# Modulation vectors of two MLP stages: from TensorE with a 32-column weight tile to VectorE with a running sum; squares of every MLP from VectorE to ScalarE

## The reference

```
silu_c, silu_cc = silu(c), silu(c_ctx)                    # two condition vectors of 1024
for i in range(4):
    sh_a, sc_a, g_a, sh_m, sc_m, g_m = split(silu_c @ mod_w[i] + mod_b[i], 6)        # mod_w[i]: 1024 x 6144
    csh_a, ... = split(silu_cc @ mod_w[i] + mod_b[i], 6)                             # layers 0 to 2 only
    h = rms_norm(x, g) * (1 + sc_a) + sh_a                # mixer: Fourier, differential attention, MLA, Fourier
    x = x + g_a * mixer(h)
    x = x + g_m * (square(relu(h2 @ mlp_w1[i])) @ mlp_w2[i])     # h2 modulated by sh_m, sc_m; hidden width 4096
```

## Time and profile before

| what | value |
|---|---|
| median of three runs | 3288.2 us (3286.24 to 3288.66) |
| the profiled execution | 3285.3 us |
| its span | 3284.0 us |
| TensorE matmul busy | 3151.4 us, 96% |
| VectorE busy | 1728.4 us, 53% |
| ScalarE busy | 1393.5 us, 42% |
| GpSimd busy | 998.6 us, 30% |
| granted TensorE clock, mean | 0.989 of 2.4 GHz |

### The profile page before, as it was taken

The page is one execution under the profiler, slowest core; times in us unless marked ns, Lnnn a source line. Parts: engine busy times, 40 slices in busy tenths (PEclk is TensorE's granted clock), DMA queues, the critical chain, the costliest instruction groups (busy, mean ns, idle before and its releaser), DMA issues.

```text
span 3284.0 us, 52135 instructions
## 1 busy us (share of the span) xinstructions
PE 3151.4 (96%) x21802; PEld 2675.0 (81%) x21802; DVE 1728.4 (53%) x3037; ACT 1393.5 (42%) x2347; POOL 998.6 (30%) x440
## 2 busy tenths in 40 slices
PE   5999999999999999999999999999999999999999
PEld 3877777776777777589989987778999978779999
DVE  3353333666543334666566556564466556554574
ACT  3442222444432223654444445554344446554443
POOL 0212113110212212134423432343434423334443
PEclk8999999999999999999999999999999999999999
DMA  9345454332355553135525542333545433325454
GB/s 290 111 155 162 155 166 154 116 103 90 105 190 167 171 175 103 54 119 189 177 79 180 179 131 74 107 95 103 173 145 184 157 103 103 103 91 164 150 180 149
DMA packets 469306, 460.07 MB, mean 140 GB/s; under 512 B 9041, under 2 KB 467665, under 8 KB 469073
## 3 DMA queue, kind: packets, MB, share of 16 engines
q1 hardware_dynamic: 465760, 453.32, 43.2%
q10 hardware_dynamic: 3312, 3.42, 0.3%
HBM read 455.66 MB, written 1.05 MB: 139 GB/s over the span
## 4 chain that ended last, share of the span: by engine, by line
PE 76%; DVE 14%; ACT 6%; issue 3%; DMA 1%; ACTq 0%; POOL 0%; DVEq 0%; SPq 0%; POOLq 0%
PE bank L400 21%; PE bank L401 20%; PE bank L402 20%; ACT wh L347 3%; DVE wl L363 3%; PE bank L444 3%; DVE hl L779 1%; DVE hidl L779 1%; DVE tmp L665 1%; PE bank L2388 1%; PE bank L563 1%; DVE xl L673 1%; DVE bc L2428 1%; PE bank L458 1%; PE bank L1250 1%
## 5 line engine op out<-in xcount | busy, mean ns | idle before, releaser
L375 POOL TENSOR_TENSOR wl<-raw,wh 128x768 fp32r<-128x768 f32 (+2 forms) x336 | 880.4, 2621 | 2101.0 <-ACT wh L347 2091.0
L347 ACT ACTIVATE wh<-raw 128x2048 fp32r<-128x2048 f32 (+1 forms) x336 | 636.4, 1894 | 315.0 <-PE bank L402 298.6
L363 DVE TENSOR_TENSOR wl<-raw,wh 128x1280 fp32r<-128x1280 f32 (+2 forms) x336 | 499.7, 1487 | 420.5 <-ACT wh L347 411.7
L400 PE MATMUL bank<-nh,wh 128*128 128x272 f32 (+1 forms) x1712 | 506.5, 296 | 6.3 <-DVE nl L1973 2.8
L402 PE MATMUL bank<-nh,wl 128*128 128x272 f32 (+1 forms) x1712 | 494.2, 289 | 0.0
L401 PE MATMUL bank<-nl,wh 128*128 128x272 f32 (+1 forms) x1712 | 492.6, 288 | 0.0
L400 PE MATMUL bank<-xh,wh 128*128 128x512 f32 (+1 forms) x1288 | 449.8, 349 | 6.9 <-DVE xl L673 3.7
L401 PE MATMUL bank<-xl,wh 128*128 128x512 f32 (+1 forms) x1288 | 437.8, 340 | 0.0
L402 PE MATMUL bank<-xh,wl 128*128 128x512 f32 (+1 forms) x1288 | 437.0, 339 | 0.0
L400 PE MATMUL bank<-hh,wh 128*128 128x512 f32 (+1 forms) x1024 | 350.3, 342 | 3.7 <-DVE X L687 1.9
L400 PEld LDWEIGHTS bank<-nh,wh 128*128 128x128 f32 x1712 | 326.7, 191 | 23.2 <-issue 19.6
(11 more groups left out here) (424 smaller groups left out, 5634.4 us busy)
## 6 DMA issues: line engine op xcount, KB each, us to landing
raw<-in_mlp_w SPq DMA_DIRECT2D x128, 1024.0 KB, 5.3
raw<-in_mod_w SPq DMA_DIRECT2D x83, 1024.0 KB, 5.2
raw<-in_w_in SPq DMA_DIRECT2D x60, 1024.0 KB, 5.2
raw<-in_w_mlp_up SPq DMA_DIRECT2D x32, 1024.0 KB, 5.5
raw<-in_w_mlp_down SPq DMA_DIRECT2D x32, 1024.0 KB, 5.0
raw<-in_w_in SPq DMA_DIRECT2D x34, 512.0 KB, 4.3
raw<-in_w_ssd_down SPq DMA_DIRECT2D x16, 1024.0 KB, 5.1
early<-in_mod_w SPq DMA_DIRECT2D x13, 1024.0 KB, 12.0
```

The lines of the kernel that those rows point to most:

```text
L347: nc.scalar.activation(self.wtile(self.wh, c1), self.rawtile(c1), AF.Copy).then_inc(*up("act_wh", ("wh", c1)))
L363: nc.vector.tensor_tensor(l, r, h.bitcast(F32), ALU.subtract).then_inc(*up("dve_wl", ("wl_dve", c1)))
L375: nc.gpsimd.tensor_tensor(l, r, h.bitcast(F32), ALU.subtract).then_inc(*up("pool_wl", ("wl_pool", c1)))
L400: nc.tensor.matmul(o, ah, bh, start=first, stop=False)
```

## The change

The 60 modulation chunks of mlp0 and mlp1 become "dmod" chunks. Their weight is read from a second copy of `mod_w`, transposed on the host (6144 x 1024), so that an output's 1024 weights lie in one partition's row; a chunk is two tiles of 128 outputs (m = 0, 1) by 1024. At the start of each of the two stages TensorE writes the condition vector, spread over all partitions, into a pair of PSUM banks (`pe_condition`, four matmuls for each half; banks 4 and 5 for `c`, banks 6 and 7 for `c_ctx`, the latter in mlp0 only, its second half after the second dense chunk). VectorE then multiplies a tile by that row and sums along it in one instruction (`scalar_tensor_tensor` with `accum_out`); in mlp0 there are two for each tile (both streams), in mlp1 one. After every second chunk VectorE adds the bias. TensorE, and ScalarE with its copy of the bank, have no part in these chunks any more.

VectorE does the chunk behind dense chunk n in its iteration of chunk n + 1, one tile before each of the two residuals or remainders. The loads alternate between `raw2` and a new 8 KB tile `extra` that lies over `mrow` and two tables that are used only later; two loads and three ScalarE places wait for the end of the other use. In mlp0 the dmod chunks follow dense chunks 0 to 27, one each; in mlp1 dense chunks 0 to 27 too, with two behind each of chunks 8 to 11.

In every MLP of the kernel (`act_mlp`, `dve_mlp`) the square moves to ScalarE: Relu, Square and copy stand one behind the other, without the delay by a group.

```diff
             if L == 0 and n < 4:
-                mods(0, 20 + n, 21 + n)
-            elif L == 1 and (n < 4 or n % 7 == 6):
-                i = 16 + n if n < 4 else 20 + n // 7
-                mods(2, i, i + 1)
-            elif L < 2 and n >= 4 and n % 7 != 6:
-                i = n - 4 - n // 7
-                mods(1 + 2 * L, i, i + 1)
+                dmods(0, 20 + n, 21 + n)
+            elif L == 0 and n < 28:
+                dmods(1, n - 4, n - 3)
+            elif L == 1 and n < 8:
+                dmods(2, 16 + n, 17 + n)
+            elif L == 1 and n < 12:
+                dmods(3, 2 * n - 16, 2 * n - 14)
+            elif L == 1 and n < 28:
+                dmods(3, n - 4, n - 3)
...
+    def dmods(layer, lo, hi):
+        for i in range(lo, hi):
+            w(("dmod", layer, i), a["mod_wT"][layer], 256 * i, 2, 0, 1024)
...
+    def pe_condition(self, st, s, half):
+        b = self.pe_bank((4 + 2 * s + half,), "cb", st, s, half)
+        for k in range(4):
+            ins = nc.tensor.matmul(b[:, 128 * k:128 * k + 128], self.cst[:, 4 * half + k, s:s + 1].broadcast_to([128, 128]), self.ident[:], start=True, stop=True)
+        ins.then_inc(*up("pe_cond", ("cb", st, s, half)))
...
+    def dve_dmod(self, c, m):
+        w = self.rawtile(c).rearrange("p (m k) -> p m k", m=2)[:, m, :]
+        DVE.wait_ge(*at("raw", c))
+        if L < 2:
+            DVE.wait_ge(*at("cb", st, 1, 0))
+            DVE.wait_ge(*at("cb", st, 1, 1))
+            nc.vector.scalar_tensor_tensor(out=self.junk[:], in0=w, scalar=1.0, in1=self.cb[1][:], op0=ALU.mult, op1=ALU.mult,
+                                           accum_out=self.modv[:, L, 2 * i + m, 1:2])
+        DVE.wait_ge(*at("cb", st, 0, 0))
+        DVE.wait_ge(*at("cb", st, 0, 1))
+        nc.vector.scalar_tensor_tensor(out=w, in0=w, scalar=1.0, in1=self.cb[0][:], op0=ALU.mult, op1=ALU.mult,
+                                       accum_out=self.modv[:, L, 2 * i + m, 0:1])
+        if m == 1 and i % 2:
+            nc.vector.tensor_tensor(dst, dst, bias, ALU.add)
...
     def pe_root(self, name, T):
-        self.pe_busy(5)
+        if name in ("mlp0", "mlp1"):
+            self.pe_condition(name, 0, 0)
+            self.pe_condition(name, 0, 1)
+            if name == "mlp0":
+                self.pe_condition(name, 1, 0)
+            self.pe_busy(1 if name == "mlp1" else 0)
+        else:
+            self.pe_busy(5)
...
     def act_hidden(self, st, i, T):
+        t = self.ring(st)[i % 4][:, T]
+        ACT.wait_ge(*at("acc", st, "h", i))
+        if i >= 4:
+            ACT.wait_ge(*at("L", st, i - 4))
+        nc.scalar.activation(t, self.place[st, "h", i][:, T], AF.Relu).then_inc(*up("act_relu", ("relu", st, i), ("out", st, "h", i)))
+        ACT.wait_ge(*at("relu", st, i))
+        nc.scalar.activation(t, t, AF.Square).then_inc(*up("act_hsq", ("hsq", st, i)))
         ACT.wait_ge(*at("hsq", st, i))
...
+                for d in dmods:
+                    self.dve_dmod(d, m)
                 if p[0] == "m1":
-                    i = waiting = 8 * p[2] + 2 * p[3] + m
-                    t = self.ring(st)[i % 4][:, T]
-                    DVE.wait_ge(*at("relu", st, i))
-                    nc.vector.tensor_tensor(t, t, t, ALU.mult).then_inc(*up("dve_hsq", ("hsq", st, i)))
+                    waiting = 8 * p[2] + 2 * p[3] + m
```

More of the change, by code:

```diff
@@ L31 @@
 EARLY = 8
+EXTRA = 8
 RING = (0, 1, 2, 3)
@@ L201, in __init__ @@
         self.ix = {p[0]: c for c, p in enumerate(self.P)}
-        self.dense = [c for c, p in enumerate(self.P) if p[0][0] != "mod"]
+        self.dense = [c for c, p in enumerate(self.P) if p[0][0] not in ("mod", "dmod")]
         self.nth = {c: d for d, c in enumerate(self.dense)}
@@ L205, in __init__ @@
         self.homes()
+        extra = [c for c in sorted(self.home) if self.home[c] == EXTRA]
+        late = [c for c in extra if c > self.ix["mod", 2, 0]]
+        self.extra_first = {extra[0]: (0, 9), late[0]: (2, 7)}
+        self.junked = None
+        self.dmod_last = [max(c for c, p in enumerate(self.P) if p[0][0] == "dmod" and (p[0][1] < 2) == first) for first in (True, False)]
+        self.extra_last = extra[len(extra) - len(late) - 1], late[-1]
         self.loaded = self.n_act = self.n_dve = self.n_pool = 0
@@ L249, in memory @@
         self.rt1 = small("rt1", 1024)
+        self.extra = self.mem("extra", 2048, F32, o[0])
+        self.mrow = [small(f"mrow{i}", 512) for i in range(2)]
         self.ckh = small("ckh", 512, F32R)
@@ L287, in homes @@
         self.home, self.prev, last = {}, {}, {}
+        dmods = [c for c in mods if self.P[c][0][0] == "dmod"]
         for c in range(len(self.P)):
@@ L470, in act_mod @@
             ACT.wait_ge(*at("acc", "modT", *self.pairs[n - 2]))
+        if L == 2 and h < 2:
+            ACT.wait_ge(*at("used", self.extra_last[0]))
         nc.scalar.activation(self.mrow[n % 2][:], self.place["mod", L, h][:], AF.Copy).then_inc(*up("act_row", ("row", L, h), ("out", "mod", L, h)))
@@ L712, in pe_mlp @@
                         self.pe_group(c, m, slot, X, T, (st, "h", i + m), m == 1)
-                        self.pe_turn()
-            else:
+                if i == 2 and st == "mlp0":
+                    self.pe_condition(st, 1, 1)
+            elif p[0] == "m2":
                 slot = self.pe_take(c)
@@ L742, in act_mlp @@
                 if p[0] == "m1":
-                    i = waiting = 8 * p[2] + 2 * p[3] + m
[L744 to L748, removed]
+                    self.act_hidden(st, 8 * p[2] + 2 * p[3] + m, T)
                 elif p[2] == 3 and nxt:
@@ L1686, in act_latent_high @@
         keys, T, g, dim, parts = self.latent(u)
+        ACT.wait_ge(*at("used", self.extra_last[1]))
         for n, (H, L) in enumerate(parts):
```

66 lines of the change are left out of this document (41 added, 25 removed).

## The result

| | before | after |
|---|---|---|
| median | 3287.4 us (3286.24 to 3288.66) | 3180.8 us (3177.12 to 3182.03) |
| profiled execution | 3285.3 us, span 3284.0 | 3179.84 us, span 3178.5 |
| ratio of the runs | | 0.9674, 95% interval 0.9657 to 0.9691 |

The change made the kernel 106.6 us faster. On a second and a third chip the ratio was 0.9675 and 0.9670.

What follows compares the result with a forecast made beforehand. TensorE was taken as the bound, busy in every microsecond of mlp0 and mlp1. 87.6 (TensorE) + 8 (small MLPs) = 95.6 off 3285.3 gives 3189.7; plus 2.9 for the median, 3192.6, say 3193 us; range 3184 to 3218.

Steps and rivals of the forecast that it cites:

- The modulation off TensorE: mlp0 and mlp1: taking modulation chunks off TensorE removes 40.2 and 46.2 us, together 86.4; net TensorE gain 87.6 us.
- 86.4 + 2.4 - 1.2 = 87.6: TensorE in mlp0 and mlp1: 86.4 us removed, 2.4 saved at the stage ends, 1.2 added by `pe_condition`.
- the count from single rows: mlp0: 27 chunks and 13 transpositions give 29.4 + 4.7 = 34 us without late starts, taken as lower bound.
- the 40.2: mlp0: 42.0 us of the stretch not dense work, less 1.8 for the first chunk, which stays.
- VectorE can take it: mlp0 and mlp1: a new sum takes 1.3 us (bounds 1.2 and 2.6); m1 chunks of mlp0 ask 9.3 of 10.88.
- The square in the small MLPs: Four small MLPs: the square on ScalarE ends VectorE's lag; 8 us saved of 10.6 in which PE is not busy.
- My upper bound: Four small MLPs: at most 10.6 us saved, the time PE is not busy in the four stretches.
- the stated range: Whole kernel: 3184 to 3218 us, holding the forecast, rival 2, the small-MLP bounds and part of the way to rival 1.
- Rival 1: mlp0: running sum takes a column twice, 2.4 us each; VectorE bounds, 48 lost after 20 of lookahead; 3241 us; chance 0.10.
- rival 3: mlp0: slower than before, from 2.8 us per new instruction; at 3.0 the loss is 115, time 3308; chance 0.05.
- Rival 2: Small MLPs: square on ScalarE gives nothing, waits come from loads or GpSimd; 3193 + 8 = 3201 us; chance 0.19.

## Why the prediction was right or wrong

**The modulation off TensorE: right.** Forecast 86.4 + 2.4 - 1.2 = 87.6; the two stages lost 88.3. Taking the term from the whole stretch less the dense matmuls was right; the count from single rows, 34 in mlp0, would have been 6 short, because the matmuls behind each insertion start late. In the kernel before, the second dense matmul behind a chunk starts 0.34 after the first and behind a transposition 0.31, instead of 0.23: 4 us over the 40 insertions, and smaller delays behind it make the rest. (The 34 is 85% of the 40.2, not 77% as the prediction has it; nothing was worked out from that share.)

**VectorE can take it: right.** Forecast 1.3 us for a sum, measured 1.22 and 83 ns for the readout, 1.14 from start to start; VectorE was busy 237 us in mlp0 where 274 were forecast. The difference of 37 is half the remainders, 32 at 0.73 on the mean instead of 1.31 (19), and half the sums, 112 at 1.14 instead of 1.3 (18). GpSimd took no turns with the new instruction. Cutting the sums away gained nothing.

**The square in the small MLPs: the step that failed.** The prediction said: "In the four stretches PE is not busy in 738.00 - 727.36 = 10.6 us. ... I take 8; bounds 10.6 and minus 5". The mechanism was right, VectorE's pace of 6.46 against 5.76, and all of it went; the size was wrong. The term measured 14.3 in the trace and 14.4 in the kernel with the squares alone. Of the 6.3 that are missing, 2.6 are the step from 10.6 down to 8, "most of the 10.6", for which the prediction has no number, and 3.7 are the reading of the loss from PE's idle time. A matmul's recorded duration is 0.28 us when the next starts 0.12 later, so the records overlap the first part of every wait, and the second matmul behind a wait starts 0.22 after the first: 0.45 idle beside 0.70 lost. My upper bound was therefore no bound. The chunk starts had the right number: 6.46 - 5.76 for each chunk that waits, and 1.2 for the last of them. The waits lie where the prediction had them, around the turn from m1 to m2.

**What is left.** Forecast and measured execution are 3189.7 and 3179.8 apart by 9.9: 6.3 from that term, 0.7 from mlp0 and mlp1, and 2.9 from stages that the change does not touch. The last can come from single executions: the second trace of the kernel before is 2.6 shorter with no change. But something like them recurs: the medians on three chips are 106.6, 107.5 and 108.8 apart, where the six MLP stages give 102.6. The three traces of the changed kernel spend 61 to 68 us at 1.2 GHz, the two of the kernel before 69 and 72; whether the change brings that about is open. I had given the clock no width in the range. For the medians 1.9 more come in: I added 2.9 for their distance to the profiled execution, and after the change it was 1.0. With the term right the forecast would have been 3192.6 - 6.3 = 3186.3, inside the stated range and still 5.5 above the measured 3180.8. All the deviations went the same way, 11.8 in all, and the term of the squares is over half of them.

**The rivals.** Rival 1 (a column twice) and rival 3 fall with 1.22 us for a sum. The experiment with doubled sums shows that rival 1 was also priced too low: about 7 us of lag are absorbed, not 20, which would make it some 61 instead of 48 (an estimate). Rival 2 (nothing in the small MLPs) falls with the kernel that has only the squares.

## What to carry to other kernels

Where an engine is busy all through a stage, work taken off it is worth the full stretch; where it waits for others, it can be worth little: 60 chunks out of the MLPs gave 88 us, eight out of the attention stage 0 to 6, since longer waits and more time at the lower clock took back most of their 10.2. Price a wait of TensorE by how far the starts behind it slip, not by the idle time in the record. A value that goes to another engine and back within one iteration can set the pace of two in-order queues while both are half idle; here the whole chain on one engine gave 14.4 us, while changing only the order of the copy lost 17.

## What the runs showed of the hardware

- VectorE's multiply with a running sum over 128 x 1024 fp32 takes 1216 ns with the second operand in PSUM or in SBUF alike, and its readout 83 or 77 ns. With two SBUF operands it takes turns with GpSimd (up to 2885 ns), with one in PSUM in none of 176 instances (at most 1222), 83 of which ran beside a GpSimd instruction.
- The place of the low-clock stretches changes between executions of one program: the first mixer took 169.4 to 170.2 us in traces where the first of them was 6.8 us long, and 170.8 to 172.1 where it was 10.2. In the attention stage each 3.4 us at 1.2 GHz made it 1.4 to 1.6 us longer (304.60, 306.0 to 306.1 and 307.6 to 307.7 at 0, 3.4 and 6.8 us).
